# Values and gates computed token-major during the norm, q turned, and squares of q and k summed on ScalarE

## What is computed

```python
h = rmsnorm(x, norm_g)
proj = jnp.einsum('bld,de->ble', h, w_in)          # 1024 -> 4104 columns
# columns: q k v (512 each, through a short convolution and SiLU), z_a (512), a and b (4 + 4, the gates),
#          the window's q k v (512 each), z_b (512)
qkv = causal_short_conv(x_ext, conv_w)
qa = l2normalize(qa) * DN_DK ** -0.5;  ka = l2normalize(ka)     # over 128 channels of a head
g = -jnp.exp(a_log) * jax.nn.softplus(a_in + dt_bias);  beta = jax.nn.sigmoid(b_in)
o_a = rmsnorm(gated_delta_rule(qa, ka, va, g, beta, s0), dn_norm_g) * jax.nn.silu(z_a)
o_b = merge_dilations([dilated window attention of (qb, kb, vb), three dilations]) * jax.nn.silu(z_b)
y = x + concat(o_a, o_b) @ w_out                    # then the final rmsnorm
```

## Time and profile before

| | us |
|---|---|
| median of 3 runs (2122.8 to 2127.5) | 2127.3 |
| the profiled execution | 2122.2 |
| its span | 2120.5 |
| PE busy | 1860.6 (88%) |
| DVE busy | 750.6 (35%) |
| ACT busy | 594.5 (28%) |
| POOL busy | 316.3 (15%) |

### The profile page before, as it was taken

One profiled execution on the slowest core, in us unless ns is written; L12 is line 12 of the kernel. 1 busy time (PEld: TensorE's weight loads), 2 busy tenths in 40 slices (PEclk: granted clock), 3 DMA queues, 4 the chain that ended last, 5 costly groups with the idle time before them and its releaser, 6 DMA issues. The chain is left out here.

```text
span 2120.5 us, 29031 instructions
## 1 busy us (share of the span) xinstructions
PE 1860.6 (88%) x9742; PEld 1461.5 (69%) x9742; DVE 750.6 (35%) x1785; ACT 594.5 (28%) x1246; POOL 316.3 (15%) x351
## 2 busy tenths in 40 slices
PE   5799999999999999952858988998899557999997
PEld 4588888888888888822647877887787434565663
DVE  6641135113411341104655344444443332322331
ACT  5421132113211321111132434443445211222221
POOL 0000000000000000012313224223423331121210
PEclk9899999999999999976969888988899659999998
DMA  5223322343342122349973887797767465666460
GB/s 169 55 69 91 95 75 61 103 98 61 73 101 90 61 80 92 93 45 240 276 212 111 276 253 235 241 291 227 241 195 229 114 196 125 189 188 178 131 181 25
DMA packets 258408, 310.76 MB, mean 147 GB/s; under 512 B 69276, under 2 KB 209052, under 8 KB 248812
## 3 DMA queue, kind: packets, MB, share of 16 engines
q1 hardware_dynamic: 254708, 242.20, 43.1%
q10 hardware_dynamic: 3584, 66.98, 8.8%
HBM read 229.55 MB, written 146.44 MB: 177 GB/s over the span
## 5 line engine op out<-in xcount | busy, mean ns | idle before, releaser
L249 PE MATMUL pj<-hT_hi,w_hi 128*128 128x512 f32 (+1 forms) x1056 | 426.6, 404 | 13.9 <-DVE w_lo L446 13.4
L250 PE MATMUL pj<-hT_lo,w_hi 128*128 128x512 f32 (+1 forms) x1056 | 415.8, 394 | 0.0
L251 PE MATMUL pj<-hT_hi,w_lo 128*128 128x512 f32 (+1 forms) x1056 | 415.3, 393 | 0.0
L249 PEld LDWEIGHTS pj<-hT_hi,w_hi 128*128 128x128 f32 (+1 forms) x1056 | 197.5, 187 | 60.1 <-DVE w_lo L446 13.8
L251 PEld LDWEIGHTS pj<-hT_hi,w_lo 128*128 128x128 f32 (+1 forms) x1056 | 197.1, 187 | 47.4 <-issue 1.2
L250 PEld LDWEIGHTS pj<-hT_lo,w_hi 128*128 128x128 f32 (+1 forms) x1056 | 197.7, 187 | 42.1 <-issue 0.9
L1381 PE MATMUL o_ps<-pt,vt 128*65 128x256 f32 (+3 forms) x560 | 151.2, 398 | 3.6 <-issue 2.1
L587 POOL IOTA row_at<- 128x1 int32 x1 | 0.1, 139 | 943.2 <-POOLq L2373 943.2
L1450 ACT ACTIVATE pt<-pt_ps 128x512 f32<-128x512 f32 x144 | 84.5, 587 | 148.3 <-PE pt_ps L1359 147.6
L2137 PE MATMUL y_bank<-wo_hi,mh 128*128 128x512 f32 (+1 forms) x272 | 112.0, 412 | 7.3 <-POOL ml L2122 5.3
L457 DVE SCALAR_TENSOR_TENSOR acc<-raw,conv_wt,acc 128x512 f32<-128x512 f32 x144 | 108.2, 752 | 9.1 <-DVE acc L454 0.3
(11 more groups left out here) (417 smaller groups left out, 3121.7 us busy)
## 6 DMA issues: line engine op xcount, KB each, us to landing
out_dram<-in_cache_k_win_dram ACTq DMA_DIRECT2D x56, 584.0 KB, 7.1
out_dram<-in_cache_v_win_dram ACTq DMA_DIRECT2D x56, 584.0 KB, 6.0
w_raw<-in_w_in_dram SPq DMA_DIRECT2D x35, 512.0 KB, 7.2
qk_ch<-sil SPq DMA_DIRECT2D x32, 256.0 KB, 2.4
z_ch<-xr SPq DMA_DIRECT2D x32, 256.0 KB, 2.4
wqk<-hi SPq DMA_DIRECT2D x32, 256.0 KB, 2.6
wqk<-lo SPq DMA_DIRECT2D x32, 256.0 KB, 3.0
out_dram<-xr SPq DMA_DIRECT2D x32, 256.0 KB, 2.8
```

Of the source, the lines that this page charges most:

```text
L249: pe.matmul(out, w_hi[s][:, k, 0:m], hT_hi[:, k, cols], start=(k == 0), stop=False)
L250: pe.matmul(out, w_hi[s][:, k, 0:m], hT_lo[:, k, cols], start=False, stop=False)
L251: mm = pe.matmul(out, w_lo[s][:, k, 0:m], hT_hi[:, k, cols], start=False, stop=(k == KT - 1))
```

## The change

**Token tiles.** The window's v (`wv`) and the gates' columns leave the loop. Their 520 columns are kept as two streaming operands `wt_hi`, `wt_lo`, in two halves of 264 and 256 columns, and 128 tokens of `hT_hi` or `hT_lo` are stationary: `token_tile(n)` makes 128 tokens by 520 columns of 8 x 3 x 2 matmuls, in two banks, as soon as x tile n is turned, with the next x tiles turned in between, five ahead. ScalarE copies the rows to `stage` and `ab_tok` (`rows_out_of`), SP stores `new_v` directly. x has three slots now. The sample rows get a tile of their own, and their v rows are stored here and not in `sample`.

**The loop** has 7 kinds, and is written out on all engines. q is turned as well, though not stored; ScalarE sums the squares of q and k over the channels from the token-major copy `tok`, four activations with an accumulator per chunk (`squares`), in place of Square and the matmuls with ones. The sample product uses the split weights: per block one fp32r matmul of 64 stationary columns (hi and lo of the 32 rows) and one of 32; a small matmul with `sam_fold` adds the halves and turns them.

**The end** with the gates' weight tile is gone.

```diff
-KINDS = ("q", "k", "v", "za", "wq", "wk", "wv", "zb")
+KINDS = ("q", "k", "v", "za", "wq", "wk", "zb")
 ...
-TURNED = ("k", "v", "wk", "wv")
+POSTED = ("q", "k", "v", "wk")
 ...
-        XS = 4
+        XS = 3
+        AHEAD = 5
 ...
+            wt_hi, wt_lo = (early.enter_context(nc.sbuf_tensor(n, [P, KT, SW_WIDTH + AB], F32R)) for n in ("wt_hi", "wt_lo"))
 ...
+        t_ps = [(pj[0], pj[1]), (pj[2], pj[3])]
 ...
+            def load_columns(g, at):
+                at_least(sp, w_lo_done, g - 1)
+                src = D.w_in[:, at:at + P].rearrange("(k p) c -> p k c", p=P)
+                sp.dma_start(w_raw[:, g % 2], src).then_inc(w_loaded[g % 2], 16)
+
+            def load_w(t):
+                j, y = divmod(t, NK)
+                load_columns(NJ + t, P * j + COLS[y])
+
+            def load_x(n):
                 if n >= XS:
                     sp.wait_ge(xT_done, 2 * (n - XS) + 2)
-                sp.dma_start(x_slot[n % XS], D.x[P * n:P * n + P, :]).then_inc(x_loaded[n % XS], 16)
-                if n == 0:
-                    sp.dma_start(g_row, D.norm_g.unsqueeze(0).to_broadcast([P, D_MODEL])).then_inc(g_in_row, 16)
-                if n in (XS, XS + 2):
-                    load_w(0, (n - XS) // 2)
-            sp.wait_ge(xT_done, 2 * (NT - XS) + 2)
-            sp.dma_start(x_slot[0][0:NS, :], D.x_sample).then_inc(x_loaded[0], 16)
+                if n < NT:
+                    sp.dma_start(x_slot[n % XS], D.x[P * n:P * n + P, :]).then_inc(x_loaded[n % XS], 16)
+                else:
+                    sp.dma_start(x_slot[n % XS][0:NS, :], D.x_sample).then_inc(x_loaded[n % XS], 16)
 ...
+            def store_rows(n):
+                sp.wait_ge(t_out, n + 1)
+                sp.dma_start(D.new_v[P * n:P * n + P, :], stage[:, n % 2, :]).then_inc(stage_stored[n % 2], 16)
 ...
+            load_columns(0, COL_WV)
+            load_columns(1, COL_WV + P)
+            load_x(2)
+            with nc.allow_non_contiguous_dma(reason="the eight columns of the gates, once"):
+                sp.dma_start(ab_raw[:], D.w_in[:, O_AB:O_AB + AB].rearrange("(k p) c -> p k c", p=P)).then_inc(ab_in, 16)
+            load_columns(2, COL_WV + 2 * P)
+            load_x(3)
+            load_columns(3, COL_WV + 3 * P)
+            load_x(4)
+            load_x(5)
+            load_w(0)
 ...
+            for n in range(8, NT + 1):
+                load_x(n)
+                store_rows(n - 8)
+            load_w(1)
+            for n in range(NT - 7, NT):
+                store_rows(n)
 ...
-            sp.wait_ge(w_lo_done, W_CREDIT + NTILES + 1)
-            sp.dma_start(w_raw[:, 0], D.w_in[:, O_AB:O_AB + P].rearrange("(k p) c -> p k c", p=P)).then_inc(w_loaded[0], 16)
 ...
+            parts = ((0, HALF + AB), (HALF + AB, SW_WIDTH + AB))
+
+            def token_tile(n):
+                if n == 0:
+                    pe.wait_ge(w_lo_done, NJ)
+                    pe.wait_ge(ab_lo_done, 1)
+                pe.wait_ge(hT_lo_done, 2 * n + 2)
+                at_least(pe, t_out, n - 1)
+                rows = slice(P * n, P * n + P)
                 for k in range(KT):
-                    pe.matmul(out, w_hi[s][:, k, 0:m], hT_hi[:, k, cols], start=(k == 0), stop=False)
-                    pe.matmul(out, w_hi[s][:, k, 0:m], hT_lo[:, k, cols], start=False, stop=False)
-                    mm = pe.matmul(out, w_lo[s][:, k, 0:m], hT_hi[:, k, cols], start=False, stop=(k == KT - 1))
-                return mm
-
-            def sam_product(s, m=P):
-
+                    for h, w in ((hT_hi, wt_hi), (hT_hi, wt_lo), (hT_lo, wt_hi)):
+                        for x, (a, z) in enumerate(parts):
+                            mm = pe.matmul(t_ps[n % 2][x][:, 0:z - a], h[:, k, rows], w[:, k, a:z],
+                                           start=(k == 0 and h is hT_hi and w is wt_hi), stop=(k == KT - 1 and h is hT_lo))
+                mm.then_inc(t_done, 1)
+
+            def sample_tile():
 ...
+                        pe.matmul(t_ps[0][x][0:2 * NS, 0:z - a], flat(h_sam[:, k]), wt_hi[:, k, a:z], start=(k == 0), stop=False, skip_group_check=True)
+                        mm = pe.matmul(t_ps[0][x][0:NS, 0:z - a], h_sam[:, k, 0, :], wt_lo[:, k, a:z], start=False, stop=(k == KT - 1), skip_group_check=True)
+                mm.then_inc(t_done, 1)
 ...
+                    pe.matmul(p_sam[0:2 * NS, 0:P], flat(h_sam[:, k]), w_hi[s][:, k, :], start=(k == 0), stop=False, skip_group_check=True)
+                    mm = pe.matmul(p_sam[0:NS, 0:P], h_sam[:, k, 0, :], w_lo[s][:, k, :], start=False, stop=(k == KT - 1), skip_group_check=True)
                 mm.then_inc(sam_mm, 1)
 ...
+                        pe.matmul(p_sam[:, P:P + NS], sam_row[:], sam_fold[:], start=True, stop=True).then_inc(sam_turned, 1)
 ...
+            for n in range(AHEAD):
+                turn_x(n, n % XS, P)
             for n in range(NT):
-                turn_x(n, n % XS, P)
-                if n >= 5 and n % 4 == 1:
-                    if n == 5:
-                        pe.wait_ge(w_lo_done, W_CREDIT + 1)
-                    first_product(n // 4 - 1)
-            turn_x(NT, 0, NS)
-            first_product(NCH - 1)
-            pe.wait_ge(ones_done, 1)
-            pe.wait_ge(h_sam_done, 2)
-            for c in range(NCH):
-                pe.sem_inc(pj_free[c], 1)
-            pe.sem_inc(sam_free, 1)
-            kinds(0, True)
-            with pe.Fori(1, NJ) as j:
-                kinds(j, False)
-
-            pe.wait_ge(w_lo_done, W_CREDIT + NTILES + 2)
-            for c in range(NCH):
-                pe.wait_ge(pj_free[c], NTILES + 1)
-                product(pj[c][0:2 * DN_HEADS, :], 0, slice(CHUNK * c, CHUNK * (c + 1)), 2 * DN_HEADS).then_inc(pj_done, 1)
-            pe.wait_ge(sam_free, NTILES + 1)
-            sam_product(0, 2 * DN_HEADS)
-
-            pe.wait_ge(ab_evac, NCH)
-            pe.wait_ge(tok_done, TOK_CREDIT + 16 * NJ)
-            for n in range(NT):
-                mm = pe.transpose(tp[0][:, 8 * n:8 * n + 8], abT[:, n * P:(n + 1) * P], ident[0:8, 0:8])
-            mm.then_inc(ab_turned, 1)
+                token_tile(n)
+                m = n + AHEAD
+                if m <= NT:
+                    turn_x(m, m % XS, P if m < NT else NS)
+            sample_tile()
+            pe.wait_ge(h_sam_done, 5)
+            pe.wait_ge(hT_lo_done, 2 * NT)
+            pe.wait_ge(t_out, NT + 1)
+            pe.wait_ge(v_sam_out, 1)
 ...
+            def rows_out_of(n):
+                a, b = t_ps[n % 2]
+                act.wait_ge(t_done, n + 1)
+                at_least(act, stage_stored[n % 2], 16 * (n // 2))
+                act.activation(stage[:, n % 2, 0:HALF], a[:, 0:HALF], ACT.Copy)
+                act.activation(ab_tok[:, n, :], a[:, at_ab], ACT.Copy)
+                act.activation(stage[:, n % 2, HALF:], b[:, 0:HALF], ACT.Copy).then_inc(t_out, 1)
 ...
+            def squares(j, kind, c):
+                y = KINDS.index(kind)
+                act.wait_ge(tok_done, posts_before(j, kind, c) + 1)
+                for b in range(4):
+                    ins = act.activation(sq[:, c % 2, P * b:P * b + P], tok[:, c % 2, P * b:P * b + P], ACT.Square, accum_out=ssq[:, 4 * c + b, y, j:j + 1])
+                ins.then_inc(sq_done, 1)
 ...
+                        at_least(dve, sq_done, squared_before(j, back, bc))
+                        dve.tensor_copy(tok[:, bc % 2, :], tp[bc % 2][:]).then_inc(tok_done, 1)
```

More of the change, by code:

```diff
@@ new lines, in product, with sam_product @@
+            def product(out, s, cols):
+                for k in range(KT):
+                    pe.matmul(out, w_hi[s][:, k, :], hT_hi[:, k, cols], start=(k == 0), stop=False)
+                    pe.matmul(out, w_hi[s][:, k, :], hT_lo[:, k, cols], start=False, stop=False)
+                    mm = pe.matmul(out, w_lo[s][:, k, :], hT_hi[:, k, cols], start=False, stop=(k == KT - 1))
+                mm.then_inc(pj_done, 1)
+            def sam_product(s):
+                for k in range(KT):
+                    pe.matmul(p_sam[0:2 * NS, 0:P], flat(h_sam[:, k]), w_hi[s][:, k, :], start=(k == 0), stop=False, skip_group_check=True)
+                    mm = pe.matmul(p_sam[0:NS, 0:P], h_sam[:, k, 0, :], w_lo[s][:, k, :], start=False, stop=(k == KT - 1), skip_group_check=True)
@@ L330, in _ @@
-            for n in range(NT):
-                mm = pe.transpose(tp[0][:, 8 * n:8 * n + 8], abT[:, n * P:(n + 1) * P], ident[0:8, 0:8])
-            mm.then_inc(ab_turned, 1)
+                if kind == "wk":
+                    pe.wait_ge(w_f32_done, 4 * j + c + 1)
+                else:
+                    pe.wait_ge(sil_done, 4 * (3 * j + y) + c + 1)
+                at_least(pe, tok_done, posts_before(j, kind, c) - 1)
+                for b in range(4):
+                    mm = pe.transpose(tp[c % 2][:, b * P:(b + 1) * P], sil[:, c, b * P:(b + 1) * P], ident[:])
@@ L342, in norm_r @@
+            def norm_r(n, rows):
+                s = n % XS
```

(43 more changed lines are left out.)

410 lines of the change are left out of this document (202 added, 208 removed).

## The result

The changed kernel took **2058.8 us** (median of four runs, 2058.4 to 2059.5) against 2126.2 (2122.8 to 2127.5): ratio 0.9686, 95% interval 0.9669 to 0.9702. That is 67 us faster, and 22.8 us more than the 2036 that was forecast: inside the range, but just outside the forecast's own 2022 to 2056.

What follows compares the result with a forecast made beforehand. TensorE was taken to bound the loop, not the opening or end. Loop -130.2, opening +72.4, end -29.4 and sample -1 sum to -88.2, from 2122.2 to 2034.0, median 2036; own range 2022 to 2056, stated range 2020 to 2072.

Steps and rivals of the forecast that it cites:

- loop starts: Opening before the loop: wv and gates as token tiles move its start from 81.4 to an effective 153.8, +72.4 us.
- median less profiled execution: The profiled sum gives 2034.0; the median of runs stands somewhat higher, at 2036.
- The end: After the last product: 10.6 us (1.2 + 6.0 + 3.4) for the conv_tail stores, against 40 before, -29.4 us.
- The start of token tile 0: In the opening: starts at 40 us, bounds 35 and 46, after the fourth weight lands at about 30.
- The token tiles: Opening: 5.74 us each, 6.7 with the turn; 16 make 91.8 us, other engines' smaller work costing nothing.
- the second rival: The norm paces the token tiles: 9.5 us each instead of 6.7, about 2081 us; chance 0.07.
- the one of a half clock throughout: TensorE stays at half clock through the token stage: slower, about 2141 us; chance 0.03.
- The loop: Over weight tiles: 28 tiles of 23.65 us plus 64 turns of 0.46, 691.6 against 821.8, -130.2 us.
- The sample product: In each loop tile: sixteen fp32r matmuls taken at 1.2 us, bounds 0.95 and 1.85, against 1.9 before.
- The relay rival: VectorE and ScalarE bound q, k, v: 7.0 us a chunk against 5.9; priced at 28, about 2064; chance 0.13.
- The sum of 5.7 us: ScalarE per loop chunk: 3.74 waiting for the convolution, 0.7 for Silu, 1.2 squares; close to TensorE's 5.9, costed at nothing.
- Behind `project`: In `sample`, four transposes, a copy and 8 DMA issues go: -1 us (0 to -2.7).

Runs made afterwards that it cites:

- both edits together: The changed kernel with the conv_tail stores issued early and x tiles 2, 3 and 4 ahead on SP's queue: 2021.4 us, ratio 0.9498.

## Why the prediction was right and wrong

Against the forecast, in the frame of the profiled executions:

| part | forecast | measured |
|---|---|---|
| loop starts | 153.8 | 160.0 |
| loop | 691.6 | 689.0 |
| end | 10.6 | 27.3 |
| all behind `project`, against before | -1 | +4.1 |
| median less profiled execution | +2 | -0.7 |

The differences, +6.2, -2.6, +16.7, +5.1 and -2.7, add to the 22.8 us but for rounding.

The end is counted here to 876.3, the last landing; up to the first instruction of `gates` the end was 28.9 us, and the sum should have taken 41.6 and not 40 from the kernel before, which makes it 1.6 us lower.

**The end is the step that failed most.** Its mechanism was right, and stood in the forecast in so many words: what is late next is a store of single floats. The size was wrong. "The last must land (3.4 us for the like-made `conv_wt` loads)": these are loads, issued in the opening, and the stores' own row in the trace of before says 19.3; after, it is 22.0. From the first issue to the last landing the forecast had 6.0 + 3.4 = 9.4 us; it was 25.9 before and 26.0 after, although the issuing took 6.04 in the one and 2.27 in the other. The run with early stores settles that the end waited for them, with 23.9 us back; why they take that long it doesn't show.

**The start of token tile 0** was put at 40, bounds 35 and 46; it was 50.0. The step took the fourth weight's landing at about 30 as what comes last and let the x tiles follow it in 3.15 us each. The order of SP's queue says otherwise: x tile 3 stands behind weight load 2, which waits for a split, and that in turn for x tile 2, which came behind two weights. With the other order of this queue tile 0 started 13.2 us earlier. Of the ten late microseconds the stage gave some back: from 50.0 to 158.2 it took 108.2 (forecast 109.1), and the wait before the loop was 1.85, not 2.7 and a cold start. So the loop began 6.2 late.

**The token tiles** were right: with its turn a tile takes 63.97 - 57.35 = 6.62 us in the changed kernel's timeline, 6.7 forecast. The granted clock is half (0.50) from 50 to 53.4 us, which costs 1.7 us where 2 were put down, and full (1.00) from there to the end of the stage. The norm's relay does not pace them, so the second rival is out, and so is the one of a half clock throughout (0.98 in the mean).

**The loop** was right to 2.6 us: a pass of 172.1 for 172.9. The sample product came out at 0.96, at the lower of its two bounds and not at the 1.2 that was taken; that alone would be 6.7 us over 28 tiles, and some 4 of them were taken back elsewhere in the loop. The price of the squares' sums, 0.81 a group by the earlier trace rows, was confirmed from the other side, at 0.87.

**The relay rival** (0.13) is out, and by more than its refusal in the trace: twice the squares still cost the loop nothing. ScalarE's row for a chunk reads 382.13 for the raw copy, 385.71 for Silu and 1.17 us for the four squares with their reads (0.295 each, the lower of the two prices considered). The sum of 5.7 us was no bound: with the second set it would be 6.9, above the 5.9 of a chunk, and TensorE still did not stop. That the four banks and the lag of two chunks are what gives this room is the likely reason, and was not tried by itself.

**Behind `project`** 1 us was to be gained and 4.1 were lost. In seven profiled executions, of the changed kernel and of single edits to its projection, the stretch was 1181.4 to 1184.0 us (with both edits together 1188.2, where the granted clock in `mixers` stayed half for 30.7 us at one place and not 13.7), and in the two of the kernel before, with and without its stores, 1177.3 and 1178.6. So it goes with the change. About 2.2 of it is the copy that stands beside GpSimd: in `sample` the change took a copy off ScalarE, whose split of a weight then came 0.5 us earlier after its first copy of the stage, so GpSimd's followed ahead of VectorE's copy and not behind it. Moving GpSimd behind it won 2.4 us up to the store of `st` and none over the whole stretch, so the cause of the 4.1 us as a whole stays open. TensorE's granted clock is a rival that wasn't tried.

## What to carry to other kernels

When a stage that hid something goes, look up that very thing's row and take its price from there; a neighbour that looks alike can be off by a factor of nearly six. A full, gapless engine between two idle stretches means that the next gain lies in the stretches: two moves of DMA issues, without any arithmetic, gave some 37 us more on top of the 67. In one queue, put what the critical relay waits for ahead of anything whose own buffer is not yet free.

## What the hardware showed

- fp32r steps of 128 columns: 0.06 us with 64 and 32 stationary columns, against 0.12 with 128 of them. The streamed columns are the same, so with the full width it is the weight load that counts. The Trainium skill ("TensorE: Matmul & The Clock Gate", LDWEIGHTS) has its time grow with the stationary columns and not with the rows. These steps agree as to the columns (0.12 with 128, 0.06 with 64); all have 128 rows, so no run here shows the other half.
- Three stores of 1,536 single floats each, 18 KB, issued together, took 22.0 us to land in the median and 24.6 for the last, with nothing but one z store ahead of them, and 12.3 to 12.7 when issued some 25 us apart in the kernel with early stores. Loads of 1,536 single floats each took 3.4 us in the kernel before and 5.0 in the changed one. The Trainium skill ("DMA: Bandwidth & Descriptors", Rules for kernel authors) says that a non-contiguous last dimension becomes one descriptor per element, and the 4,672 packets under 512 B agree.
- A VectorE copy of 4x384 took 2.50 us beside a GpSimd tensor_tensor begun 0.2 us earlier, and 0.34 when GpSimd began after it. The Trainium skill ("GPSIMD Engine Reference", Specifications) names the SBUF interface that these engines share; here the whole of GpSimd's 2.5 us was waited out.
- Four ScalarE squares with their accumulator reads took 1.17 us, so some 0.1 of each read's 0.19 lies under the next square.
